# A new order of units, banks and cuts in the second attention of a fused two-block transformer kernel

## Chip, cores and metric

One core of a Trainium2 chip runs the whole program, one launch. The metric is the device time of one execution in microseconds. The kernel before takes 1139.63 us, the median of three runs (1139.48 to 1142.15).

## The reference

Two blocks of a transformer on 256 tokens of width 1024, float32 throughout. The first has three attentions (stick-breaking, forgetting, and one over a memory), gates and a relu-squared feed-forward. The second block has two layers. Its first layer is the one that matters here: an attention with 16 heads of 64 in 4 groups, with three branches whose outputs are gated and added.

```python
q = rms_norm(parts[0].reshape(B, T, G, HG, DH), q_norm)
kc, vc, ksl, vsl, kw, vw = [a.reshape(B, T, G, DH) for a in parts[1:7]]
...
k_cmp = rms_norm(compress(kc, pos_k, k_w1, k_b1, k_w2), kcmp_norm)   # gelu(blk @ w1 + b1) @ w2
v_cmp = compress(vc, pos_v, v_w1, v_b1, v_w2)
...
o = gb[..., 0:1] * o_c + gb[..., 1:2] * o_s + gb[..., 2:3] * o_w
...
x = x + o @ w_out
```

At 256 tokens the selected branch (o_s) and the window branch (o_w) both see every earlier position; the compressed branch (o_c) sees 15 compressed keys for each group. After it come a gated feed-forward, a second attention layer and a second feed-forward.

## The kernel before

The program is written by hand for each engine, as five instruction streams that meet at semaphores: `tensor_program`, `scalar_program`, `vector_program`, `gpsimd_program`, `sync_program`. Each stream is in order: an instruction that waits holds up all behind it on its engine. Nothing plans the order; it is the order of the text, and the loops over `i` in the four compute programs are meant to run side by side.

Weights stream through three raw buffers (`m.raw`), 1 MB a chunk, loaded by SyncE in the order of `CHUNKS`. Each chunk is cut into a rounded high part (ScalarE, `cut`) and a rest (VectorE, `cut`), and TensorE's `gemm` multiplies three pairs of high and low parts (lines 579, 581, 582). A raw buffer comes free when VectorE has cut its chunk. Chunks 84 to 87 hold the two compression weights and are used raw, by the products `hidden(n)` (line 906), 16 for the keys into bank 0 and 16 for the values into bank 1. Chunks 88 to 91 are the four blocks of the output projection `nwo`: 88 and 89 its first k half for output halves 0 and 1, 90 and 91 the second.

The attention is 32 units, in the order that `nsa_units` gives. A unit `main` computes the selected and the window branch for one head (token half 1, 256 keys) or two heads (token half 0, 128 keys); a unit `few` computes the compressed branch for four heads. Head block 0 comes first (units 0 to 11), then head block 1 (12 to 15 for token half 0, and from 16 on for token half 1), with the `few` units of block 0 placed between those of the last group.

The loop `for i in range(35)` runs in four streams:

- TensorE: in step i the scores of unit i into bank 6 or 7 (lines 663 and 674), then the transposes of the exponents of unit i-2 (line 559), then some filling work (`gemm` pieces or `hidden`), then the values of unit i-3 (line 694), then other transposes. A unit that opens an output group takes that group's bank, and waits until the group that held it has been read. In the steps of `late_opens` the values of unit i-4 and i-3 come together, a step late.
- VectorE: in step i a split or `stacked_...` where one is due, the maximum of unit i (line 1926), the copy of the transposed rows of unit i-2 out of PSUM (line 1938, every third is ScalarE's), the `join` of a group that ended with unit i-3 (reciprocal, gates, two passes that read the two output banks, one addition; in `late_joins` with unit i-4), then `hidden`, then a quarter of a `cut`.
- ScalarE: placing and splits, the exponents of unit i (line 1189), tanh, a quarter of a `cut` (line 1192).
- GpSimd: the gelu chains (`cubic`, `gelu`) and the scaling of the compressed keys.

Output groups lie in banks by `O_BANKS`: each entry is the bank of a group in the order in which the groups first appear. Transposes go through two spare banks, 4 and 5, in turn, among them `turn_out`, which transposes the joined output for the projection. Line 1769 is VectorE's helper for every tensor_tensor, 1192 ScalarE's copy, 2422 GpSimd's tensor_tensor.

Of the kernel before, what the change touches and what calls it, by code (L numbers as in the profile page):

```python
# [108 lines left out]
def bank_pairs():  # L109

    at, turn = {}, 0
    for name, kt, widths in GEMMS:
        if name in ("flog", "ngate", "cmpk", "cmpv"):
            continue
        for b in range(len(widths)):
# [7 lines left out]
            if name == "nwo":  # L123
                at[name, b] = ((3, 0), (1, 7))[b]
# [310 lines left out]
def nsa_units():  # L435
    main, few = {}, {}
# [8 lines left out]
    units = [*a, *b, *c, *d[:3], e[0], d[3], e[1], d[4], f[0], d[5], f[1], *d[6:], *g, *z]  # L445
# [19 lines left out]
O_BANKS = {"fox": (2, 3), "nsa": (2, 3, 2, 3, 2, 3, 0, 1, 2, 2, 2, 2), "mla": (2, 3)}  # L465
# [69 lines left out]
def tensor_program(e, m, book):  # L535
# [446 lines left out]
    late_opens = [u.i + 4 for u in NSA[4:] if u.kind == "main" and u.opens and u.i < 16]  # L982
    for i in range(35):
# [14 lines left out]
        elif 11 <= i < 17:  # L998
            for n in range(3 * i - 17 - max(0, i - 15), 3 * i - 14 - max(0, i - 14)):
                hidden(n)  # L1000
        elif 27 <= i < 31:
            gemm(88, lo_out, ready_out, (0,), (i - 27,))
# [17 lines left out]
        elif i in (12, 15):  # L1020
            turn_queries(1, 1, i // 15)
        elif i in (13, 19):
            turn_hidden(i // 19)
        elif i in (14, 20):
            compressed(i // 20)
        elif i == 17:
            w.wait_ge(*after("keys copied"))
            turn(("kst",), [m.kst[:]])
        elif i in (25, 29):
            turn_out(0, (i - 25) // 4)  # L1030
# [148 lines left out]
def scalar_program(e, m, book):  # L1179
# [379 lines left out]
    for i in range(35):  # L1559
# [6 lines left out]
        elif i in (13, 16):  # L1566
            place_queries(1, 1, i // 16)
        elif i in (14, 20):
            hidden(i // 20)
# [8 lines left out]
        elif i == 21:  # L1578
            w.wait_ge(*after("on", "cmp", 1))
            copy(m.vc[:], bank("cmp", 1)[0:60, 0:64]).then_inc(*out(("off", "cmp", 1)))  # L1580
        elif i in (26, 30):
            split(("no", 0, (i - 26) // 4), m.o_lo[0][:, :, half((i - 26) // 4)])
# [13 lines left out]
        elif i in (12, 18):  # L1596
            tanh(i // 18)
        if 11 <= i < 15:
            cut(88, i - 11)
        elif 20 <= i < 28:  # L1600
            cut(89 + (i - 20) // 4, (i - 20) % 4)
        elif 28 <= i < 32:
            cut(91, i - 28)
# [156 lines left out]
def vector_program(e, m, book):  # L1760
# [411 lines left out]
    for i in range(35):  # L2172
# [6 lines left out]
        elif i in (13, 16):  # L2179
            stacked_queries(1, 1, i // 16)  # L2180
        elif i in (26, 30):
            split(("no", 0, (i - 26) // 4), both(m.o_lo, 0, 4, (i - 26) // 4))
        elif i == 34:
            split(("no", 1, 0), both(m.HT, 4, 8, 0))
        if i < 32:
            maximum(NSA[i])
        if i == 18:
# [713 lines left out]
```

## Time and profile before

| | |
|---|---|
| median of three runs | 1139.63 us (1139.48 to 1142.15) |
| the profiled execution | 1142.15 us |
| its span, first to last instruction | 1140.3 us |
| TensorE matmuls busy | 1116.6 us, 98% |
| TensorE weight loads busy | 936.1 us, 82% |
| VectorE, ScalarE, GpSimd busy | 54%, 51%, 15% |
| granted TensorE clock | 0.999 |

Times in the timeline are microseconds from the span's start. A bracket at the end of a row is the time that the engine stood idle before it and the instruction that ended the wait. The ends of matmuls are modelled, and matmuls overlap, so the distance from one start to the next says more than a matmul's own duration. The loop of the second attention lies at about 548 to 650 us.

### The profile page before, as it was taken

The numbers are of one execution on the slowest core, as the hardware profiler recorded it, in microseconds if no ns is written. First come the engines' busy times: TensorE is split into PE (matmuls) and PEld (weight loads), VectorE is DVE, ScalarE is ACT, GpSimd is POOL, SyncE is SP. The second block draws the span as 40 slices with busy tenths as digits, with TensorE's granted clock in tenths as the row PEclk, the third lists the DMA queues.
The fourth block names the chain that finished last, engine by engine and source line by source line (L and its number), as shares of the span: only waits on it lengthen the run. The fifth ranks groups of instructions, "written<-read, shape, count | busy, mean of one in ns | idle before, by whom it ended". The sixth has DMA issues, their size and how long they took to land.

```text
span 1140.3 us, 14182 instructions
## 1 busy us (share of the span) xinstructions
PE 1116.6 (98%) x5899; PEld 936.1 (82%) x5899; DVE 620.1 (54%) x655; ACT 577.9 (51%) x891; POOL 171.0 (15%) x222
## 2 busy tenths in 40 slices
PE   6999999999999999999999999999999999999998
PEld 5777778888899988888878888888888687888887
DVE  5444454557645445457657665555456646555542
ACT  5688655443555534346567354444447635444431
POOL 1022111111131200032311000000017921000000
PEclk9999999999999999999999999999999999999999
DMA  9533333345554554545122255554544225555552
GB/s 340 203 116 143 147 116 144 132 166 192 202 200 166 212 184 185 189 155 185 59 98 88 75 184 184 185 184 166 184 151 162 76 111 191 187 184 191 183 170 77
DMA packets 28384, 184.34 MB, mean 162 GB/s; under 512 B 3472, under 2 KB 3856, under 8 KB 8080
## 3 DMA queue, kind: packets, MB, share of 16 engines
q1 hardware_dynamic: 26496, 177.52, 43.1%
q0 software_dynamic: 1824, 5.92, 1.5%
q8 instruction: 46, 0.75, 0.3%
q14 instruction: 18, 0.15, 0.0%
HBM read 182.38 MB, written 1.05 MB: 161 GB/s over the span
## 4 chain that ended last, share of the span: by engine, by line
PE 92%; ACT 3%; DVE 2%; POOL 2%; DMA 1%; issue 0%; POOLq 0%; DVEq 0%
PE ps L579 23%; PE ps L581 23%; PE ps L582 23%; PE ps L559 6%; PE ps L694 4%; PE ps L674 3%; PE ps L612 3%; PE ps L611 3%; PE ps L610 3%; POOL t L2422 2%; DVE t L1769 1%; ACT t L1192 1%; PE ps L906 1%; ACT t L1189 1%; DMA t<-in_g 1%; ACT L1189 1%
## 5 line engine op out<-in xcount | busy, mean ns | idle before, releaser
L1769 DVE TENSOR_TENSOR t<-t 128x2048 fp32r<-128x2048 f32 (+6 forms) x259 | 411.0, 1597 | 347.8 <-ACT t L1192 335.5
L579 PE MATMUL ps<-t 128*128 128x512 f32 (+2 forms) x1186 | 470.4, 397 | 4.0 <-DVE t L1769 2.7
L1192 ACT ACTIVATE t<-t 128x2048 fp32r<-128x2048 f32 (+5 forms) x220 | 323.5, 1485 | 278.3 <-PE ps L582 241.8
L581 PE MATMUL ps<-t 128*128 128x512 f32 (+2 forms) x1186 | 461.9, 389 | 0.6 <-POOL t L2422 0.6
L582 PE MATMUL ps<-t 128*128 128x512 f32 (+2 forms) x1186 | 462.1, 390 | 0.0
L579 PEld LDWEIGHTS ps<-t 128*128 128x128 f32 x1186 | 223.9, 189 | 48.5 <-DVE t L1769 5.1
L582 PEld LDWEIGHTS ps<-t 128*128 128x128 f32 x1186 | 223.7, 189 | 46.6
L581 PEld LDWEIGHTS ps<-t 128*128 128x128 f32 x1186 | 224.1, 189 | 44.3 <-POOL t L2422 1.1
L2422 POOL TENSOR_TENSOR t<-t 128x32 f32<-128x32 f32 (+10 forms) x127 | 122.2, 977 | 487.5 <-ACT t L1189 423.4
L1189 ACT ACTIVATE t<-ps,t 128x256 f32<-128x256 f32 (+4 forms) x216 | 95.9, 453 | 104.3 <-DVE t L1926 47.5
L559 PE MATMUL ps<-t 128*128 128x128 f32 (+3 forms) x667 | 96.4, 275 | 14.4 <-DVE t L1769 10.5
L1192 ACT ACTIVATE t<-ps 128x512 fp32r<-128x512 f32 (+8 forms) x106 | 57.3, 560 | 94.7 <-PE ps L559 89.0
L559 PEld LDWEIGHTS ps<-t 128*128 128x128 f32 (+3 forms) x667 | 77.9, 137 | 30.8 <-issue 14.1
L1769 DVE TENSOR_TENSOR t<-ps,t 128x512 fp32r<-128x512 f32 (+5 forms) x132 | 81.5, 638 | 35.1 <-ACT t L1192 31.9
L610 PE MATMUL ps<-t 128*128 128x256 f32 x256 | 72.5, 283 | 0.0
L612 PE MATMUL ps<-t 128*128 128x256 f32 x256 | 72.5, 283 | 0.0
L611 PE MATMUL ps<-t 128*128 128x256 f32 x256 | 72.4, 283 | 0.0
L1192 ACT ACTIVATE t<-ps,t 128x512 f32<-128x512 f32 (+5 forms) x75 | 44.9, 645 | 31.8 <-PE ps L559 22.4
L674 PE MATMUL ps<-t 128*128 128x256 f32 (+5 forms) x240 | 53.4, 343 | 0.3 <-DVE t L2322 0.3
L694 PEld LDWEIGHTS ps<-t 128*128 128x128 f32 (+1 forms) x384 | 46.8, 191 | 5.8 <-issue 4.5
L694 PE MATMUL ps<-t 128*128 128x64 f32 (+2 forms) x384 | 49.8, 274 | 0.0
L611 PEld LDWEIGHTS ps<-t 128*128 128x128 f32 x256 | 49.1, 192 | 0.0
(98 smaller groups left out, 536.3 us busy)
## 6 DMA issues: line engine op xcount, KB each, us to landing
t<-in_w SPq DMA_DIRECT2D x158, 1024.0 KB, 4.9
t<-in_w SPq DMA_DIRECT2D x8, 512.0 KB, 3.5
t<-in_w SPq DMA_DIRECT2D x5, 768.0 KB, 4.3
t<-in_g POOLq DMA_DIRECT2D x6, 512.0 KB, 5.7
t<-in_w SPq DMA_DIRECT2D x2, 640.0 KB, 3.8
t<-in_x SPq DMA_DIRECT2D x4, 256.0 KB, 5.9
t<-in_mem POOLq DMA_DIRECT2D x1, 1024.0 KB, 9.8
out<-t SPq DMA_DIRECT2D x4, 256.0 KB, 4.5
```

Source lines behind the costliest of these rows:

```text
L559: t = e.transpose(ps[0:n, j * 128:j * 128 + rows], s, m.ident[0:rows, 0:rows])
L579: e.matmul(o, sh, wh, start=k0 + j == 0, stop=False)
L581: e.matmul(o, sh, wl, start=False, stop=False)
L582: t = e.matmul(o, sl, wh, start=False, stop=last and j == n - 1)
L610: e.matmul(o, wh, hi, start=k == 0 and f == 0, stop=False, skip_group_check=True)
L611: e.matmul(o, wh, lo, start=False, stop=False, skip_group_check=True)
L612: t = e.matmul(o, wl, hi, start=False, stop=k == 7 and f == 1, skip_group_check=True)
L694: t = e.matmul(bank[k][:, o:o + v.shape[1]], PT[u.i % len(PT)][0:rows, z * 128:(z + 1) * 128], v, start=c == 0, stop=c == len(blocks) - 1)
L1189: return e.activation(o, src, f, **k)
L1192: return e.activation(o, src, ACT.Copy, scale=scale)
L1769: return e.tensor_tensor(o, a, b, op)
L2422: return e.tensor_tensor(o, a, b, op)
```

## The change

The order of the units: the first `few` unit moves from place 19 to 20, and the others of block 0 from 21, 23 and 25 to 22, 24 and 26. The banks: the groups of block 1, token half 1, go to banks 2 and 3 in place of 0 and 1, the compressed groups to bank 1 in place of 2, and the projection's outputs to 0, 2, 3, 7 in place of 3, 0, 1, 7. Unit 16's values become one of the late ones, in step 20. The `hidden` products of the values' compression are spread over steps 11 to 17, and what follows from them moves by a step. VectorE's stacked compressed keys come ahead of the maximum in step 18. The output transposes of block 0 and their splits move a step later. The cuts of chunks 88 to 90 now run without a pause, on ScalarE in steps 12 to 23 and on VectorE in 13 to 24, and those of chunk 91 a step earlier.

```diff
--- before.py
+++ after.py
@@ -121,7 +121,7 @@
             if name == "nsc":
                 at[name, b] = (2, 3)
             if name == "nwo":
-                at[name, b] = ((3, 0), (1, 7))[b]
+                at[name, b] = ((0, 2), (3, 7))[b]
             if name == "mwo":
                 at[name, b] = ((0, 1), (6, 7))[b]
             if name == "qa":
@@ -442,7 +442,7 @@
             few[hg, h] = [Unit("nsa", "few", 0, h, tuple(range(u0, u0 + 4)), 60, hg, 4) for u0 in (0, 4)]
     a, b, c, d = main[0, 0], main[0, 1], main[1, 0], main[1, 1]
     e, f, g, z = few[0, 0], few[0, 1], few[1, 0], few[1, 1]
-    units = [*a, *b, *c, *d[:3], e[0], d[3], e[1], d[4], f[0], d[5], f[1], *d[6:], *g, *z]
+    units = [*a, *b, *c, *d[:4], e[0], d[4], e[1], d[5], f[0], d[6], f[1], d[7], *g, *z]
     return numbered(units)
 
 
@@ -462,7 +462,7 @@
 LAST_OF_FIRST = max(u.i for u in NSA if u.block == 0)
 MLA, MLA_GROUPS = mla_units()
 S_BANKS = {"fox": lambda i: (6, 7)[i % 2], "nsa": lambda i: (6, 7)[i % 2], "mla": lambda i: (6, 7)[i % 2]}
-O_BANKS = {"fox": (2, 3), "nsa": (2, 3, 2, 3, 2, 3, 0, 1, 2, 2, 2, 2), "mla": (2, 3)}
+O_BANKS = {"fox": (2, 3), "nsa": (2, 3, 2, 3, 2, 3, 2, 3, 1, 1, 1, 1), "mla": (2, 3)}
 
 
 def queries_of(m, u, n):
@@ -979,7 +979,7 @@
     def ready_out(k, h):
         return after("off", "no", k // 4, h)
 
-    late_opens = [u.i + 4 for u in NSA[4:] if u.kind == "main" and u.opens and u.i < 16]
+    late_opens = [u.i + 4 for u in NSA[4:] if u.kind == "main" and u.opens]
     for i in range(35):
         if i < 32:
             nsa_scores(NSA[i])
@@ -995,11 +995,11 @@
         elif 7 <= i < 11:
             for n in range(4 * i - 28, 4 * i - 24):
                 hidden(n)
-        elif 11 <= i < 17:
-            for n in range(3 * i - 17 - max(0, i - 15), 3 * i - 14 - max(0, i - 14)):
+        elif 11 <= i < 18:
+            for n in range(2 * i - 6 + max(0, i - 16), min(2 * i - 4 + max(0, i - 15), 32)):
                 hidden(n)
-        elif 27 <= i < 31:
-            gemm(88, lo_out, ready_out, (0,), (i - 27,))
+        elif 28 <= i < 31:
+            gemm(88, lo_out, ready_out, (0,), ((0,), (1,), (2, 3))[i - 28])
         elif i == 31:
             gemm(89, lo_out, ready_out, (0,))
         elif i == 33:
@@ -1017,17 +1017,17 @@
             turn_queries(0, 1, i - 2)
         elif i in (9, 10):
             turn_queries(1, 0, i - 9)
-        elif i in (12, 15):
-            turn_queries(1, 1, i // 15)
-        elif i in (13, 19):
-            turn_hidden(i // 19)
-        elif i in (14, 20):
-            compressed(i // 20)
+        elif i in (12, 16):
+            turn_queries(1, 1, i // 16)
+        elif i in (13, 20):
+            turn_hidden(i // 20)
+        elif i in (14, 21):
+            compressed(i // 21)
         elif i == 17:
             w.wait_ge(*after("keys copied"))
             turn(("kst",), [m.kst[:]])
-        elif i in (25, 29):
-            turn_out(0, (i - 25) // 4)
+        elif i in (26, 30):
+            turn_out(0, (i - 26) // 4)
     gemm(90, lo_out, ready_out, (0,))
     turn_out(1, 1)
     gemm(91, lo_out, ready_out, (0,))
@@ -1563,10 +1563,10 @@
             place_queries(0, 1, i - 3)
         elif i in (10, 11):
             place_queries(1, 0, i - 10)
-        elif i in (13, 16):
-            place_queries(1, 1, i // 16)
-        elif i in (14, 20):
-            hidden(i // 20)
+        elif i in (13, 17):
+            place_queries(1, 1, i // 17)
+        elif i in (14, 21):
+            hidden(i // 21)
         elif i == 15:
             o = bank("cmp", 0)[0:60, 0:64]
             w.wait_ge(*after("on", "cmp", 0))
@@ -1575,11 +1575,11 @@
         elif i == 18:
             w.wait_ge(*after("on", "kst"))
             copy(m.cA[:], bank("kst")[:, 0:60], m.cst("gnc")).then_inc(*rounded(("stacked", "kst")))
-        elif i == 21:
+        elif i == 22:
             w.wait_ge(*after("on", "cmp", 1))
             copy(m.vc[:], bank("cmp", 1)[0:60, 0:64]).then_inc(*out(("off", "cmp", 1)))
-        elif i in (26, 30):
-            split(("no", 0, (i - 26) // 4), m.o_lo[0][:, :, half((i - 26) // 4)])
+        elif i in (27, 31):
+            split(("no", 0, (i - 27) // 4), m.o_lo[0][:, :, half((i - 27) // 4)])
         elif i == 34:
             split(("no", 1, 0), m.HT[0][:, 4:8, half(0)])
         if 2 <= i < 34 and i - 2 in TURNED_BY_ACT:
@@ -1593,14 +1593,12 @@
                 copy(m.KD[i - 1][0:64, :, half(h)], p[0:64]).then_inc(*out(("off", "dup", i - 1, h)))
         elif i in (3, 5):
             squares_by_head("nsq1", 0, i // 4, 512)
-        elif i in (12, 18):
-            tanh(i // 18)
-        if 11 <= i < 15:
-            cut(88, i - 11)
-        elif 20 <= i < 28:
-            cut(89 + (i - 20) // 4, (i - 20) % 4)
-        elif 28 <= i < 32:
-            cut(91, i - 28)
+        elif i in (12, 19):
+            tanh(i // 19)
+        if 12 <= i < 24:
+            cut(88 + (i - 12) // 4, (i - 12) % 4)
+        elif 27 <= i < 31:
+            cut(91, i - 27)
     split(("no", 1, 1), m.HT[0][:, 4:8, half(1)])
     cut_by_piece(92)
     split_half("f1", 0, 0)
@@ -2176,21 +2174,21 @@
             stacked_queries(0, 1, i - 3)
         elif i in (10, 11):
             stacked_queries(1, 0, i - 10)
-        elif i in (13, 16):
-            stacked_queries(1, 1, i // 16)
-        elif i in (26, 30):
-            split(("no", 0, (i - 26) // 4), both(m.o_lo, 0, 4, (i - 26) // 4))
-        elif i == 34:
-            split(("no", 1, 0), both(m.HT, 4, 8, 0))
-        if i < 32:
-            maximum(NSA[i])
-        if i == 18:
+        elif i in (13, 17):
+            stacked_queries(1, 1, i // 17)
+        elif i == 18:
             p, a = bank("kst")[:, 0:60], m.cA
             w.wait_ge(*after("stacked", "kst"))
             e.tensor_copy(m.cB[0:64], bm(a[low_k].bitcast(F32), 2)).then_inc(*out(("copied",)))
             w.wait_ge(*after("copied"))
             e.scalar_tensor_tensor(out=a[low_k], in0=p[low_k], scalar=m.cst("gnc")[low_k], in1=a[low_k].bitcast(F32),
                                    op0=ALU.mult, op1=ALU.subtract).then_inc(*rests(("off", "kst")))
+        elif i in (27, 31):
+            split(("no", 0, (i - 27) // 4), both(m.o_lo, 0, 4, (i - 27) // 4))
+        elif i == 34:
+            split(("no", 1, 0), both(m.HT, 4, 8, 0))
+        if i < 32:
+            maximum(NSA[i])
         if 2 <= i < 34 and i - 2 not in TURNED_BY_ACT:
             copy_rows(NSA[i - 2], m.PT1)
         for n in (i - 3, i - 4):
@@ -2219,14 +2217,12 @@
         elif i == 8:
             w.wait_ge(*after("blocks", 0))
             scale_queries(1, 1)
-        elif i in (11, 17):
-            hidden(i // 17)
-        if 12 <= i < 16:
-            cut(88, i - 12)
-        elif 21 <= i < 29:
-            cut(89 + (i - 21) // 4, (i - 21) % 4)
-        elif 29 <= i < 33:
-            cut(91, i - 29)
+        elif i in (11, 18):
+            hidden(i // 18)
+        if 13 <= i < 25:
+            cut(88 + (i - 13) // 4, (i - 13) % 4)
+        elif 28 <= i < 32:
+            cut(91, i - 28)
     add_and_gain_half("nwo", 0, 0, "f1", G_FF0, ("no", 0, 0))
     split(("no", 1, 1), both(m.HT, 4, 8, 1))
     cut_by_piece(92)
```

## Rows read from the trace of the kernel before

**Rows 1.** The page's first part: busy us, share of the span, count, by engine

```profile
PE 1116.6 (98%) x5899; PEld 936.1 (82%) x5899; DVE 620.1 (54%) x655; ACT 577.9 (51%) x891; POOL 171.0 (15%) x222
```

**Rows 2.** Busy time by stretch: us, then by engine, clock, DMA share, GB/s

```profile
548.00:620.00 72.00, 71.98 (x507) 58.54 (x506) 47.51 (x86) 46.16 (x170) 15.52 (x25) 1.00 0.25 87
620.00:650.00 30.00, 28.80 (x191) 24.21 (x190) 19.46 (x39) 11.94 (x50) 0.00 (x0) 1.00 0.25 93
```

**Rows 3.** Timeline of TensorE's matmuls, steps 27 and 31 (start, us, line, shape)

```profile
619.81 0.28 PE L663 MATMUL ps<-t 128*128 128x256 bf16 x1
...
620.98 0.63 PE L559 MATMUL ps<-t 128*60 128x128 f32 x4 [0.42 <-DVE t L1769]
...
632.69 0.27 PE L663 MATMUL ps<-t 128*128 128x240 bf16 x1
...
633.61 0.62 PE L559 MATMUL ps<-t 128*60 128x128 f32 x4
635.01 0.50 PE L579 MATMUL ps<-t 128*128 128x512 f32 x1 [0.78 <-DVE t L1769]
```

**Rows 4.** Timeline of TensorE's matmuls, steps 11 and 16 to 19

```profile
576.01 1.51 PE L906 MATMUL ps<-t 128*60 128x256 f32 x6
...
593.81 0.60 PE L559 MATMUL ps<-t 128*128 128x128 f32 x4
594.35 1.07 PE L906 MATMUL ps<-t 128*60 128x256 f32 x4
595.35 2.00 PE L694 MATMUL ps<-t 128*128 128x64 f32 x16
...
599.34 0.28 PE L663 MATMUL ps<-t 128*128 128x256 bf16 x1
...
599.93 0.60 PE L559 MATMUL ps<-t 128*128 128x128 f32 x4
600.37 1.00 PE L694 MATMUL ps<-t 128*128 128x64 f32 x8
601.21 0.27 PE L663 MATMUL ps<-t 128*128 128x240 bf16 x1
...
602.23 0.66 PE L559 MATMUL ps<-t 128*128 128x128 f32 x4
```

**Rows 5.** Timeline of VectorE, steps 15, 17, 18, 26 and 30

```profile
592.61 0.24 DVE L2158 RECIPROCAL t<-t 128x16 f32<-128x16 f32 x1
...
593.10 1.29 DVE L1769 TENSOR_TENSOR t<-ps,t 128x512 f32<-128x512 f32 x2
...
599.28 0.42 DVE L1769 TENSOR_TENSOR t<-ps,t 60x256 f32<-60x256 f32 x1
600.13 0.69 DVE L1926 TENSOR_REDUCE t<-ps 128x2 f32<-128x512 f32 x1 [0.43 <-PE ps L674]
600.74 0.22 DVE L2190 CAST t<-t 64x120 fp32r<-64x120 f32 x1
...
601.18 0.67 DVE L1938 COPY t<-ps 128x512 f32<-128x512 f32 x1
...
620.23 0.69 DVE L1769 TENSOR_TENSOR t<-ps,t 128x512 fp32r<-128x512 f32 x1 [1.75 <-ACT t L1192]
...
633.18 0.23 DVE L2158 RECIPROCAL t<-t 128x16 f32<-128x16 f32 x1
...
633.67 1.29 DVE L1769 TENSOR_TENSOR t<-ps,t 128x512 f32<-128x512 f32 x2
```

**Rows 6.** Timeline of ScalarE, step 18

```profile
599.60 0.31 ACT L1192 ACTIVATE t<-ps,t 128x60 fp32r<-128x60 f32 x1
```

**Rows 7.** Timeline of GpSimd, the last step of the second gelu

```profile
602.75 0.72 POOL L2422 TENSOR_TENSOR t<-t 60x256 f32<-60x256 f32 x1
```

**Rows 8.** DMA issues from 570 to 660 us: count, KB each, us to landing

```profile
t<-in_w SPq DMA_DIRECT2D x8, 1024.0 KB, 4.8
```

## The prediction

> **What bounds the kernel now.** The summary comes first [rows 1]: TensorE is counted busy for 98% of the span, VectorE and ScalarE for about half. So the change, which touches only the order of the second attention (the 35 steps of `for i in range(35)`), can gain only what TensorE waits there. The table of stretches [rows 2] covers these steps: TensorE's matmuls are busy for 71.98 of 72 us in the first stretch and 28.80 of 30 in the second, at a clock of 1.00. The missing 1.2 us are the two brackets in the timeline of matmuls [rows 3]: 0.42 in front of transposes, 0.78 in front of block 89, both released by a VectorE tensor_tensor.
>
> Since a modelled end can hide a wait, I price by the distance from one start to the next [rows 3]. The four transposes of step 27 start 1.17 us after the scores of the step began (619.81 to 620.98), where step 18 has 0.59 (599.34 to 599.93 [rows 4]): 0.58 us waited. The bank they want still holds the first output transposes, which VectorE's split leaves at 620.23 plus 0.69, and that split had itself waited 1.75 us for ScalarE's half [rows 5]. In step 31 block 89 starts 1.40 us after the transposes (633.61 to 635.01), where four transposes take 0.44 (599.93 to 600.37): 0.96 us. It takes a bank that VectorE's join of unit 27 frees at 633.67 plus 1.29 [rows 5]. Together some 1.6 us, the whole known stock of waits that this change could win.
>
> The Trainium skill (Perfetto Trace Analysis, Identifying the Most-Contended Engine) says that matmul busy time is a poor measure of how near TensorE is to its limit and that weight-load busy time is a better one. Here the weight loads are busy for 82.75 of 102 us [rows 2], so by that rule up to 19 us would be open rather than 1.6.
>
> **The change, part by part.** The matrix work is the same in kind and count: 32 units of scores, transposes and values, 32 `hidden` products, projection blocks 88 to 91. Only places move.
>
> (a) The second `hidden` run is spread over seven steps (11 to 17: 2,2,2,2,2,3,3) instead of six (3,3,3,3,2,2). Three products take 1.51 us and two take 1.07 [rows 4], so 0.44 for one; two with all that belongs to them last from 594.35 to 595.35, so 0.12 are a run's own. The transposes ahead of a run take 0.54 (593.81 to 594.35) instead of 0.44 (599.93 to 600.37). One run more costs 0.12 + 0.10, some **+0.2 us**. The lighter steps 11 to 15 start sooner by a product each, and so do the maxima and the late join of unit 11, which frees banks 2 and 3 at 593.10 plus 1.29 in before [rows 5], 0.96 us ahead of the values at 595.35. In after, the query transposes leave step 15 for step 16 behind the values, and the two hidden products of step 16 become three, so join and values both come earlier by about as much. Nothing there; if that margin were gone, the loss would stand in step 16, and its bounds are 0 and 0.5 (the transposes that left).
>
> (b) Block 1's second half now accumulates in banks 2 and 3, which its first half (unit 15 the last) still holds, and opens at step 20 (`late_opens` gains 20). Before, it opened banks 0 and 1 in step 19 and waited for nobody. VectorE still joins unit 15 in step 19. TensorE's side of the walk [rows 4]: step 19 started at 601.21, now at 601.4 by (a). Full scores take 0.59 (599.34 to 599.93), transposes 0.44, and no values follow: 602.4. Step 20: the small scores take 0.92 (632.69 to 633.61 [rows 3]), then transposes 0.44: at 603.8 it asks for banks 2 and 3.
> VectorE's side [rows 5]: the stacked keys of step 18 go first now. ScalarE's copy of them ends at 599.91 [rows 6], and both VectorE operations take 0.44 (600.74 to 601.18): about 600.4. Maximum 0.61 (600.13 to 600.74): 601.0. Copy of rows, 0.6 when the next stands behind it (its row says 0.67): 601.6. Then `hidden`, 0.42, moved here from step 17: 602.1. Then a quarter of the cut of block 89, moved here from step 22, a 512-column pass like the copy, 0.6: 602.7. Step 19: maximum 0.61, 603.3; the join frees both banks 1.78 us after its start (592.61 to 593.10 plus 1.29): 605.1. So TensorE waits 605.1 - 603.8, a new wait: **+1.3 us**. It is 0.6 if VectorE comes to the join with no backlog (602.0 + 0.61 + 1.78 = 604.4), and 2.5 if the cuts of steps 16 and 17 and the later query placing (two passes of 0.6) leave VectorE one pass or two further behind. What is queued behind the join on VectorE is the cut of step 19 and the maximum of unit 20; its exponents and transposes are due on TensorE only in step 22, two steps later, and a step is 1.9 (0.59 + 0.44 + 0.84, the last from 600.37 to 601.21) to 2.2 us, so no second wait follows. The gelu chain took in before 3.8 us, from the end of VectorE's `hidden` at 599.70 to GpSimd's last product at 602.75 plus 0.72 [rows 7]. From 602.1 that is 605.9. TensorE asks for it in step 20 behind the values of units 16 and 17, at 605.1 + 1.7 = 606.8, and finds it done; were the banks free it would ask at 605.5 and wait 0.4 instead.
>
> The Trainium skill (Perfetto Trace Analysis, Optimizing Tensor Performance, Matmuls) says that independent groups should rotate through different PSUM banks, so that emptying one overlaps the next. Part (b) ends one such rotation, and the walk gives it a price of the same sign; by the rule alone, without a duration, only the sign would be known.
>
> (c) The first small unit moves from 19 to 20, and the stacked keys come before the maximum. In before its scores took 1.02 us (601.21 to 602.23 [rows 4]) against the 0.92 of a later one, while VectorE did the keys: **-0.1 us**.
>
> (d) Output transposes move from steps 25 and 29 to 26 and 30, their splits to 27 and 31, and the cuts of blocks 89 to 91 to four or one step earlier. Between the first output transposes and the next user of their bank lies now one small scores (0.92) in place of a full one (0.59): 0.3 us more cover. VectorE waited for ScalarE's half, which in before had a cut ahead of it in step 25 and has none now. Of the 0.58 us I take **-0.5** (bounds 0 and -0.6). In step 30 VectorE no longer has the second split (0.69 as the first) ahead of the maximum and the join. The join of unit 27 can't start before its values end at 632.69 [rows 3], and it started at 633.18 [rows 5]: **-0.45** (bounds 0 and -0.5). The rest of that wait, 0.5, is the join itself, which block 89 still needs. Block 88's first half goes in three runs rather than four, in the same count of matmuls; a run's own cost in (a) bounds it at -0.1, and I take nothing.
>
> (e) SyncE: the raw buffers of blocks 92 to 94 come free with the cuts, one to four steps earlier, and block 90's with the last `hidden`, one step later. Transfers land 4.8 us after issue [rows 8] and block 90 is cut from step 20 on, three steps (some 6 us) after step 17. No wait of TensorE in these stretches is on a transfer. Nothing; were that cover gone, ScalarE would be 1 or 2 us late with block 90, which TensorE reads only after step 34.
>
> Sum: 0.2 + 1.3 - 0.1 - 0.5 - 0.45 = **+0.45 us**, on a profiled execution of 1142.15 us (span 1140.3, 1.85 around it). The median of the three runs is 1139.63, 2.5 lower than the profiled one, and the difference goes on the median: **1140.1 us**.
>
> **The rivals.** *The waits only move* (forecast): about 1 us either way of +0.45. Under 0.3% (3.4 us, about what a measurement of this kernel can tell from no change), so it counts as the same.
> *VectorE falls behind in steps 16 to 20* and TensorE waits in 20 and again after it. For it: the cuts now run without a pause from 13 to 24, and step 18 puts 0.44 + 0.61 + 0.6 + 0.42 + 0.6 = 2.7 us on VectorE against TensorE's 1.9. Against: from step 20 VectorE has 1.2 to 1.8 us a step (two or three passes of 0.6) against 1.9 to 2.2 for TensorE, so the lag is worked off. Price: 2.5 for the bank and no gain in the tail, +0.2: +2.7, 1142.3. It decides from 0.8 us more, that is if the gelu chain, which ScalarE's tanh shares with exponents that come late, ends past 607.6 rather than at 605.9: then 1143.1 and beyond, slower.
> *Faster*: the bank wait is covered and both tail waits vanish whole: 0.2 - 0.1 - 1.6 = -1.5, 1138.1, still the same by the bound. Only by hidden waits could it be faster by more than 3.4 us: a fifth of the 19 us in which weight loads stand still, giving 1136.2 or less. Against it: the same kinds of work take nearly the same distance in different steps [rows 3, 4] (0.92 and 1.02 for small scores, 0.44 to 0.54 for transposes) but for the two waits named, which hidden waits of differing length would not leave so.
> *Nothing of the order matters*, since the same products bind TensorE: 1139.6.
>
> **How the numbers follow.** Waits only move, or nothing matters: 0.86. VectorE behind, within the bound: 0.04, past it: 0.05. Faster beyond the bound: 0.03; -1.5 us: 0.02. So faster 0.03, same 0.92, slower 0.05. The bounds of the parts give -0.5 (0.2 + 0.6 - 0.1 - 0.6 - 0.5 - 0.1) to +3.1 (0.2 + 2.5 - 0.1 + 0.5). The three runs themselves spread from 1139.48 to 1142.15, and I let the low end reach the -1.5 case and stop the high end at the rival's +2.7. Range: 1138.0 to 1142.3.
>
> **What would show it.** In the new profile TensorE should show one wait of 0.6 to 2.5 us before the values of the 17th unit (a run of sixteen L694 matmuls, the first in banks 2 and 3), released by VectorE's tensor_tensor; the wait for the bank of the first output transposes gone or under 0.2, that before block 89 near 0.5. `hidden` products should stand in eleven runs. Wrong would be: no wait at step 20, a wait on ScalarE or GpSimd's gelu of over 1 us, or starts in steps 11 to 16 that widen.

## The result

The changed kernel takes 1156.78 us (median of 4; 1155.03 to 1159.22), the kernel before 1140.14 beside it (median of 4). The ratio is 1.0144, with a 95% interval of 1.0117 to 1.0172: slower by 16.6 us, where 0.5 was forecast.

### The profile page after: what moved, and what is told of

It reads as the page before. It is cut to its first block, busy times and chain, and to the rows that moved or that the text cites. A ratio compares the mean times of both kernels' runs of the same rounds, so it can differ in the third digit from the quotient of the medians.

```text
span 1153.4 us, 14184 instructions
## 1 busy us (share of the span) xinstructions
PE 1128.9 (98%) x5899; PEld 947.1 (82%) x5899; DVE 620.8 (54%) x655; ACT 578.4 (50%) x891; POOL 171.7 (15%) x222
## 4 chain that ended last, share of the span: by engine, by line
PE 92%; ACT 3%; DVE 2%; POOL 2%; DMA 1%; issue 0%; SPq 0%; POOLq 0%; ACTq 0%; DVEq 0%
PE ps L579 22%; PE ps L582 22%; PE ps L581 22%; PE ps L559 6%; PE ps L694 4%; PE ps L674 3%; PE ps L612 3%; PE ps L610 3%; PE ps L611 3%; POOL t L2418 2%; ACT t L1192 1%; PE ps L906 1%; DVE t L1767 1%; ACT t L1189 1%; DMA t<-in_w 1%; PE ps L663 1%
## 5 line engine op out<-in xcount | busy, mean ns | idle before, releaser
L1767 DVE TENSOR_TENSOR t<-t 128x2048 fp32r<-128x2048 f32 (+5 forms) x259 | 411.3, 1598 | 347.5 <-ACT t L1192 335.8
L579 PEld LDWEIGHTS ps<-t 128*128 128x128 f32 x1186 | 223.5, 188 | 48.0 <-DVE t L1767 4.9
L582 PEld LDWEIGHTS ps<-t 128*128 128x128 f32 x1186 | 223.2, 188 | 46.4
L581 PEld LDWEIGHTS ps<-t 128*128 128x128 f32 x1186 | 223.6, 189 | 44.1 <-POOL t L2418 1.1
L559 PE MATMUL ps<-t 128*128 128x128 f32 (+3 forms) x667 | 99.9, 282 | 13.3 <-DVE t L1767 9.4
L559 PEld LDWEIGHTS ps<-t 128*128 128x128 f32 (+3 forms) x667 | 80.5, 141 | 29.9 <-issue 14.1
L694 PEld LDWEIGHTS ps<-t 128*128 128x128 f32 (+1 forms) x384 | 52.9, 212 | 8.0 <-issue 4.7
L674 PE MATMUL ps<-t 128*128 128x256 f32 (+5 forms) x240 | 57.8, 364 | 0.3 <-DVE t L2318 0.3
L694 PE MATMUL ps<-t 128*128 128x64 f32 (+2 forms) x384 | 55.9, 296 | 1.3 <-DVE t L1767 1.3
L1924 DVE TENSOR_REDUCE t<-ps 128x2 f32<-128x512 f32 (+2 forms) x48 | 30.7, 640 | 36.2 <-PE ps L674 35.9
```

Of the source, the lines that this page charges most:

```text
L559: t = e.transpose(ps[0:n, j * 128:j * 128 + rows], s, m.ident[0:rows, 0:rows])
L579: e.matmul(o, sh, wh, start=k0 + j == 0, stop=False)
L581: e.matmul(o, sh, wl, start=False, stop=False)
L582: t = e.matmul(o, sl, wh, start=False, stop=last and j == n - 1)
L694: t = e.matmul(bank[k][:, o:o + v.shape[1]], PT[u.i % len(PT)][0:rows, z * 128:(z + 1) * 128], v, start=c == 0, stop=c == len(blocks) - 1)
L1767: return e.tensor_tensor(o, a, b, op)
```

## The profile after

The page of the changed kernel, its span, its busy time by engine and the granted clock in 40 slices:

```profile
span 1153.4 us, 14184 instructions
...
PE 1128.9 (98%) x5899; PEld 947.1 (82%) x5899; DVE 620.8 (54%) x655; ACT 578.4 (50%) x891; POOL 171.7 (15%) x222
...
PEclk9999999999999999999995999999999999999999
```

Beside [rows 1], TensorE has 12.3 us more busy time for the same 5899 matmuls, and VectorE and ScalarE have the same as before within 1 us. So TensorE did not wait 13 us longer: its work took longer. One slice of the granted clock, in tenths of full speed, says 5; a slice is 28.8 us (1153.4 over 40).

The table of stretches of the same kernel, cut where the clock changes (us, busy time of TensorE, weight loads, VectorE, ScalarE, GpSimd, then clock, DMA share and GB/s):

```profile
548.00:604.40 56.40, 54.27 (x360) 41.71 (x360) 36.32 (x68) 35.17 (x121) 13.01 (x24) 1.00 0.30 105
604.40:635.10 30.70, 30.70 (x139) 27.46 (x138) 14.31 (x25) 12.20 (x53) 0.91 (x1) 0.50 0.20 69
635.10:650.00 14.90, 14.84 (x109) 13.22 (x109) 9.92 (x21) 7.91 (x34) 0.00 (x0) 1.00 0.00 1
```

For 30.7 us TensorE has half its clock, 1.2 GHz in place of 2.4, and is busy the whole time. In [rows 2] the clock is 1.00 over the whole loop. Below, the work of this loop is called narrow: transposes of 128 columns, values of 64 and small scores of 60, with wider full scores (one matmul of 256 columns, two of 512) only in about every second step. Wide stands for matmuls of 512 columns back to back. What stands ahead of the fall is in the timeline of matmuls, steps 19, 20 and 27:

```profile
599.66 0.60 PE L559 MATMUL ps<-t 128*128 128x128 f32 x4
601.08 0.28 PE L663 MATMUL ps<-t 128*128 128x240 bf16 x1 [0.81 <-ACT t L1189]
...
602.01 0.66 PE L559 MATMUL ps<-t 128*128 128x128 f32 x4
603.95 3.17 PE L694 MATMUL ps<-t 128*128 128x64 f32 x16 [1.29 <-DVE t L1767]
607.05 0.47 PE L559 MATMUL ps<-t 60*128 60x60 f32 x2
...
632.24 1.06 PE L559 MATMUL ps<-t 128*128 128x128 f32 x4
633.09 0.42 PE L663 MATMUL ps<-t 128*128 128x256 bf16 x1
...
635.15 1.11 PE L694 MATMUL ps<-t 60*128 60x64 f32 x8
```

TensorE stands still twice in step 20. From the transposes of step 19 to the small scores it is 1.42 us, of which the transposes take 0.44: 0.98 us for the exponents of unit 18. From the transposes of step 20 to the sixteen value matmuls it is 1.94, of which transposes there take 0.49 (602.23 [rows 4] to 602.72, where that timeline has values next): 1.45 us for the join of unit 15. The sixteen matmuls themselves start at the full clock and end at the half one (3.17 us, 2.00 in [rows 4]). From then on eight value matmuls take 1.8 us instead of 1.0.

VectorE and ScalarE ahead of the two waits:

```profile
594.27 1.25 ACT L1192 ACTIVATE t<-ps,t 128x512 fp32r<-128x512 f32 x2
597.07 0.48 ACT L1189 ACTIVATE t<-ps,t 128x256 f32<-128x256 f32 x1 [1.55 <-DVE t L1924]
...
597.98 0.63 ACT L1192 ACTIVATE t<-t 128x512 fp32r<-128x512 f32 x1
598.50 0.31 ACT L1192 ACTIVATE t<-ps,t 128x60 fp32r<-128x60 f32 x1
600.00 0.47 ACT L1189 ACTIVATE t<-ps,t 128x256 f32<-128x256 f32 x1 [1.19 <-DVE t L1924]
```

```profile
595.55 0.76 DVE L2061 SCALAR_TENSOR_TENSOR t<-ps,t 64x512 fp32r<-64x512 f32 x1 [2.79 <-ACT t L1192]
596.34 0.69 DVE L1924 TENSOR_REDUCE t<-ps 128x2 f32<-128x512 f32 x1
...
597.66 0.69 DVE L1767 TENSOR_TENSOR t<-t 128x512 fp32r<-128x512 f32 x1
598.85 0.21 DVE L2182 CAST t<-t 64x120 fp32r<-64x120 f32 x1 [0.49 <-ACT t L1192]
...
599.29 0.68 DVE L1924 TENSOR_REDUCE t<-ps 128x2 f32<-128x512 f32 x1
...
602.02 0.23 DVE L2156 RECIPROCAL t<-t 128x16 f32<-128x16 f32 x1
...
602.52 1.29 DVE L1767 TENSOR_TENSOR t<-ps,t 128x512 f32<-128x512 f32 x2
```

The delay builds up in three stages. VectorE idles 2.79 us until ScalarE has placed the last queries (594.27 plus 1.25), whose transposes now stand behind the values of step 16. So the maximum of unit 17 (596.34) and the exponents behind it (597.07) are late. Then a quarter of a cut (597.98) stands ahead of ScalarE's copy of the stacked keys, which ends at 598.81 (598.50 plus 0.31). Only then does VectorE go on to the keys and, at 599.29, the maximum of unit 18. The exponents start at 600.00, and the join frees the banks at 603.81.

## The experiments

Theory A: the waits of step 20 lower TensorE's clock, and the narrow matmuls of this loop then run at half speed until something denser comes. Theory B: the new order itself, narrow work massed together, lowers it. Below, a standstill is a distance between two starts less the time that the same work takes without a wait.

**banks_back**, the change with the banks and the opening step undone:

```diff
-O_BANKS = {... "nsa": (2, 3, 2, 3, 2, 3, 2, 3, 1, 1, 1, 1) ...}
+O_BANKS = {... "nsa": (2, 3, 2, 3, 2, 3, 0, 1, 2, 2, 2, 2) ...}
-late_opens = [u.i + 4 for u in NSA[4:] if u.kind == "main" and u.opens]
+late_opens = [u.i + 4 for u in NSA[4:] if u.kind == "main" and u.opens and u.i < 16]
```

> The changed kernel with one part undone: the output groups of block 1, token half 1, lie in banks 0 and 1 again, the compressed groups in 2, the projection in 3, 0, 1, 7, and unit 16 opens in step 19 again. Everything else of the change stays. Theory A (the wait for banks 2 and 3 in step 20 lets TensorE's granted clock fall to 1.2 GHz, and the narrow matmuls of this loop then run at half speed for some 30 us): no wait of over 0.5 us at steps 19 and 20, the clock stays at 1.00 from 560 to 650, and the time is that of the kernel before or up to 1 us less, 1139 to 1140.5. Theory B (the new order itself, with narrow work massed in steps 19 to 26 and fewer wide products in steps 11 to 15, lowers the clock): it still falls, 1153 to 1158.

Measured: 1153.72 us, ratio 1.0117 (1.0098 to 1.0136). My expectation of theory A, that without the new banks there is no wait, was wrong. Its timeline of matmuls:

```profile
600.39 1.10 PE L694 MATMUL ps<-t 128*128 128x64 f32 x8 [0.67 <-DVE t L1767]
...
604.81 0.33 PE L559 MATMUL ps<-t 60*128 60x60 f32 x2 [1.06 <-POOL t L2418]
...
606.28 0.66 PE L559 MATMUL ps<-t 128*128 128x128 f32 x4 [0.46 <-DVE t L1936]
```

TensorE waits for bank 1, which VectorE's `hidden` leaves late, then for the gelu chain behind it, then for a spare bank. The clock falls 0.6 us after the last of the three and is low for 23.9 us. The banks decide only what TensorE waits for. This run doesn't part theory B from A.

**banks_only**, the same edit the other way round on the kernel before (new banks and step 20, nothing else).

> The kernel before with that one part of the change alone: the new banks and unit 16 in step 20; order of units, cuts and hidden products as before. Theory A: TensorE waits for the join of unit 15 in step 20, but VectorE comes to it with less behind it (no cut and no hidden product in steps 17 to 19), so the wait is 0.5 to 1.5 us instead of 1.5 plus 1.0; if that is enough for the clock to fall the time is 1150 to 1158, if not it is 1140 to 1141. Theory B: no fall, 1140 to 1141.

Measured: 1140.29 us (10 executions), ratio 1.0008 (0.9994 to 1.0021).

```profile
598.93 0.66 PE L559 MATMUL ps<-t 128*128 128x128 f32 x4
600.22 0.33 PE L559 MATMUL ps<-t 60*128 60x60 f32 x2 [0.63 <-POOL t L2422]
...
601.07 0.60 PE L559 MATMUL ps<-t 128*128 128x128 f32 x4
601.68 1.97 PE L694 MATMUL ps<-t 128*128 128x64 f32 x16
```

0.80 us are lost to the gelu chain (1.29 less 0.49) and 0.17 to the join (0.61 less 0.44). In the profiled execution the clock stays, as at the lower end of what theory A allowed. Three others had mean clocks of 0.997 (1145.41 us) and 0.998 (1143.32 and 1142.72), where no execution of before was under 0.999. So they had shorter falls somewhere; where, no profile shows.

**filler**, the whole change, with TensorE working where it waited:

```diff
+    def fill(n):
+        for _ in range(n):
+            e.matmul(bank[0], m.identb[:], m.maskb[:, 0:512], start=True, stop=True, skip_group_check=True)
     for i in range(35):
+        if i == 20:
+            fill(4)
...
+        if i == 20:
+            fill(6)
         if i in late_opens:
```

> The whole change, and in step 20 ten more matmuls of 512 bf16 columns into the free bank 0, four ahead of the small scores and six ahead of the values of unit 16, so that TensorE works in the place of its two waits; their results are used by nobody. Theory A: the clock stays at 1.00, and the time falls from 1156 to 1139 plus the waits and what the fillers add, 1140 to 1143. Theory B: the narrow stretch that follows is unchanged, so the clock falls all the same, 1155 to 1160.

Measured: 1141.29 us (10 executions, 1140.25 to 1143.08), ratio 1.0009 (1.0000 to 1.0019).

```profile
602.21 0.66 PE L559 MATMUL ps<-t 128*128 128x128 f32 x4
602.70 1.46 PE L984 MATMUL ps<-t 128*128 128x512 bf16 x6
604.14 1.97 PE L694 MATMUL ps<-t 128*128 128x64 f32 x16
```

The values of unit 16 start 1.93 us after the transposes, against 1.94 in the changed kernel, and VectorE's join frees the banks at 604.00, 0.14 us ahead of them, as in the changed kernel: the dependencies are as late as they were. But the sixteen matmuls take 1.97 us, and the clock stays at 1.00 for the whole loop. The same order of narrow work with the standstill filled costs at most 0.2%. So the order alone doesn't lower the clock, and theory B falls, with one reservation: the filling is itself wide work. A filling of narrow matmuls was not run, so whether any work in that place would do is not shown. That a standstill by itself is enough, without the new order, is what the next runs test.

**one_wait**, the kernel before with one wait of TensorE added:

```diff
+        if i == 19:
+            w.wait_ge(*after("off", "o", 1, 0, 2))
         if i in late_opens:
```

> The kernel before, with one wait added and nothing else: TensorE waits in step 19, ahead of the values of unit 16, until VectorE has read the outputs of unit 15 in its join, some 2.1 us after it would have gone on (602.7 to 604.8). Theory A: the clock falls within a few us of it and stays low for 25 to 40 us; 1150 to 1158. Theory B: the wait costs its own length, 1141 to 1142.5, clock 0.999.

Measured: 1154.94 us, ratio 1.0132 (1.0104 to 1.0160). The profile has the values of step 19 at 602.32 behind transposes at 599.66, 2.2 us of standstill, and the clock low for 27.3 us. One wait alone, and none of the change, costs 15.0 us, nearly what the change costs (16.6), and the two intervals overlap.

**pause_short** and **pause_long**, the kernel before with a pause in step 22, of two or seven tiny GpSimd operations:

```diff
+        if i == 22:
+            w.wait_ge(*after("paused"))
         if i in late_opens:
...
     gelu(1)
+    pause(("on", "P", "nsa", 20))
     rms("nwo")
```

> The kernel before, with one pause: in step 22 TensorE waits, after its transposes, for GpSimd to run two tiny operations (8 columns) that start when those transposes end. About 0.7 to 1.0 us of standstill in the narrow stretch, no part of the change. If the length of standstill in a narrow stretch decides (theory A): about that of banks_only (0.6 and 0.2 us, no fall), so the clock stays in most executions, 1140.5 to 1141.5, perhaps falls in some. If any standstill does it: 1150 to 1158.

> The same with seven operations in place of two: 2.0 to 2.7 us of standstill in step 22. Theory A: the clock falls soon behind it and comes back only about where the projection blocks run, some 20 to 30 us later; 1150 to 1157. Rival (what fell in step 20 had to do with the banks, the join or the exponents, not with the standstill): no fall, 1142 to 1143.

Measured: 1148.36 us (6 executions, 1144.52 to 1154.36), ratio 1.0071 (1.0044 to 1.0099), for the short one, and 1148.18 (4 executions), ratio 1.0072 (1.0049 to 1.0095), for the long one. The first fence is of pause_short, the second of pause_long:

```profile
607.12 0.60 PE L559 MATMUL ps<-t 128*128 128x128 f32 x4
608.72 1.10 PE L694 MATMUL ps<-t 60*128 60x64 f32 x8 [1.00 <-POOL t L2600]
```

```profile
609.74 1.10 PE L694 MATMUL ps<-t 60*128 60x64 f32 x8 [2.39 <-POOL t L2600]
...
623.11 1.06 PE L559 MATMUL ps<-t 128*128 128x128 f32 x4
623.97 0.42 PE L663 MATMUL ps<-t 128*128 128x256 bf16 x1
...
624.80 0.60 PE L559 MATMUL ps<-t 128*128 128x128 f32 x4
```

Both medians are 8 us above the kernel before, 1140.19 beside them. That is more than the standstills alone and less than the 10 us or more that the expectations had for a fall. The standstills are 1.1 us (1.60 less the 0.54 of such transposes [rows 4]) and 2.5 (2.99 less 0.54). The clock was low for 17.1 and 13.7 us. It fell at about 611 in both and came back at 628.4 and 624.5. So the equal times are made of different parts: of 8 us, the short pause is 1.1 and the slow work 7, the long pause 2.5 and the slow work 5.5. In these two profiles the longer standstill did not make the slow stretch longer, and in both the slow work costs more than the standstill. What comes on top of the standstill is the narrow work between the fall and the place of return. In pause_long that place, 624.5, lies behind the output transposes and full scores, as in the changed kernel (632.24 to 635.1); in pause_short it is one step later. Why there and not at earlier full scores, no run parts.

**pause_wide**, the long pause among matmuls of 512 columns, between chunks 104 and 105.

> The same seven operations, but the pause stands in the gated feed-forward behind this attention, between chunks 104 and 105, among matmuls of 512 columns. Theory A with its second half (what costs is not the fall but that the narrow work behind it does not bring the clock back): the clock falls in some or all executions, for 3 to 7 us, and the time is 1142 to 1147. If a fall always lasts 30 us: 1155 and more. If it depends on nothing but the pause's own length: 1142.

Measured: 1142.35 us (10 executions, 1140.96 to 1146.23), ratio 1.0019 (1.0007 to 1.0031), so 2.2 us, about the pause's own 1.8:

```profile
732.30 0.60 PE L559 MATMUL ps<-t 128*128 128x128 f32 x4
734.48 0.50 PE L579 MATMUL ps<-t 128*128 128x512 f32 x1 [1.58 <-POOL t L2600]
```

In the profiled execution the clock didn't fall there. Three others had mean clocks of 0.997 and 0.998, so short falls are likely in some. The time alone also fits a pause that costs only its own length.

The same profile has a fall of 3.4 us elsewhere, in the last attention of the program:

```profile
892.63 3.65 PE L674 MATMUL ps<-t 128*128 128x128 f32 x16 [0.32 <-DVE t L2324]
896.21 0.79 PE L579 MATMUL ps<-t 128*128 128x512 f32 x1
```

Ahead of it stand sixteen scores of 128 columns and a wait of only 0.32 us. The clock fell at 895.6 and came back at 899.0. The profiles of banks_back and cuts_back have the same at 907, behind the same scores. So not every fall has a standstill of about a microsecond ahead of it. What led to these three was not tested.

**cuts_back**, the change with blocks 89 to 91 cut in their old steps:

```diff
-        if 12 <= i < 24:
-            cut(88 + (i - 12) // 4, (i - 12) % 4)
+        if 12 <= i < 16:
+            cut(88, i - 12)
+        elif 20 <= i < 28:
+            cut(89 + (i - 20) // 4, (i - 20) % 4)
```

and in the same way on VectorE, a step later, and for block 91.

> The whole change, but the cuts of blocks 89 to 91 stand in the steps they had in the kernel before, so none on ScalarE from 16 to 19 nor on VectorE from 17 to 20. TensorE's two waits in step 20 (1.0 us for the exponents of unit 18, 1.5 us for the join) should shrink by some 0.5 and 0.9 us, to about 1.1 in all. Theory A: between banks_only (0.8 us in all, no fall) and the change (2.5, fall), so either mostly 1140 to 1141, or falls in part of the executions, spread from 1140 to 1155. If the cuts have no part in it: both waits and the fall stay, 1153 to 1157.

Measured: 1154.57 us (4 executions), ratio 1.0127 (1.0098 to 1.0156). The wait for the exponents is gone and the join's is 1.0 us (1.49 less 0.49). The clock falls all the same, for 27.3 us in the profile, and in all four executions. So the cuts made the wait for the exponents and part of the join's, but without them enough is left. The expectation had named either mostly no fall or one in part of the executions.

```profile
600.41 0.66 PE L559 MATMUL ps<-t 128*128 128x128 f32 x4
601.90 2.46 PE L694 MATMUL ps<-t 128*128 128x64 f32 x16 [0.84 <-DVE t L1769]
```

**cuts_only**, the kernel before with the new steps of the cuts alone.

> The kernel before with the new steps of the cuts alone (ScalarE 12 to 23 and 27 to 30, VectorE one later). Theory A: each quarter of a cut puts 0.5 to 0.6 us on ScalarE and VectorE in steps 17 to 20. The exponents of unit 18, the gelu chain and its transposes come later by up to 1.2 us, and the gelu transposes of step 19, which found their input only 0.2 us old, wait 0.5 to 1.5 us. A fall then, 1148 to 1157. If only the banks and the unit order make waits: 1139 to 1140.5.

Measured: 1139.70 us (10 executions), ratio 1.0000 (0.9990 to 1.0010). The fall that I expected isn't there: the gelu transposes wait 0.16 us and a later set 0.4. The cuts alone make no standstill that matters.

**mended**, cuts_back with the last query transposes in step 15 again:

```diff
-        elif i in (12, 16):
-            turn_queries(1, 1, i // 16)
+        elif i in (12, 15):
+            turn_queries(1, 1, i // 15)
```

> The change with the old steps for the cuts of blocks 89 to 91 and the last query transposes back in step 15, ahead of the values of units 12 and 13. In cuts_back the one wait left, 1.05 us for the join of unit 15, still brought the clock down; VectorE's stacked queries (0.6 us) and what waits for them come earlier now, so the wait should shrink to 0.3 to 0.6 us. Theory A: no fall, and of the change the shorter waits at the end of the loop remain: 1138.8 to 1140, at best 0.1% under the kernel before. If the wait stays near 1 us: 1150 to 1156.

Measured: six executions, 1141.61, 1142.35, 1155.86, 1155.92, 1159.14 and 1160.66 us. The profiled one is the first; its clock is 1.00 in this loop, with this wait:

```profile
602.83 0.65 PE L559 MATMUL ps<-t 128*128 128x128 f32 x4
604.20 1.97 PE L694 MATMUL ps<-t 128*128 128x64 f32 x16 [0.72 <-DVE t L1769]
```

0.9 us of standstill (1.37 less 0.49), where 0.3 to 0.6 was expected. The same program falls in four executions and doesn't in two. The four are known by their times and by granted clocks of 0.984 to 0.979 over the span, against 0.999. None of the four was profiled, so it isn't shown that their standstill was 0.9 us too.

**rewarm**, the whole change with its waits, and `fill(12)` in step 21, when the clock is low.

> The whole change with its waits and its fall, and twelve matmuls of 512 bf16 columns into the free bank 0 in step 21, when the clock is low; their results are used by nobody, they cost 5.1 us at 1.2 GHz. Theory A, second half (narrow work does not bring the clock back, wide back-to-back work does): the clock is back by about 614 instead of 635, which gives back some 10 us and costs 3 to 5: 1148 to 1152. If a fall has a fixed length of 14 to 30 us: 1159 to 1163.

Measured: 1149.57 us (4 executions), ratio 1.0078 (1.0061 to 1.0095), 7 us under the change.

```profile
604.35 3.48 PE L694 MATMUL ps<-t 128*128 128x64 f32 x16 [1.29 <-DVE t L1774]
...
610.05 3.41 PE L984 MATMUL ps<-t 128*128 128x512 bf16 x12
613.30 1.00 PE L694 MATMUL ps<-t 128*128 128x64 f32 x8
```

In this execution, the fastest of the four (1147.19 us), the clock was low for 6.8 us instead of 30.7. It came back at 611.4, within the wide matmuls, and the narrow ones behind them run at full speed. A fall has no fixed length. The other three had mean clocks of 0.993 and 0.994, against 0.997 here, so theirs was low for longer; how it went there, no profile shows.

**mended_fill**, mended with `fill(4)` ahead of the values of unit 16.

> mended, whose executions fell into two groups (1141.6 and 1142.4 without a fall in this loop, 1155.9 to 1160.7 with one), and four matmuls of 512 bf16 columns into the free bank 0 ahead of the values of unit 16, which take up the 0.9 us that TensorE stood still there; their results are used by nobody. Theory A: no execution falls, all in 1138.5 to 1143, ratio to the kernel before 0.999 to 1.001, since of the change only some 0.5 us of shorter waits at the loop's end are left. If something else than the standstill parts mended's executions: two groups again.

Measured: 1140.02 us (12 executions, 1138.62 to 1142.64), ratio 1.0006 (0.9998 to 1.0015). No execution of the upper group is left. So the fall of mended's four executions hung on the place where TensorE stood still, with the same reservation on wide work as for filler. It is also the best version of the new order, and it doesn't beat the kernel before.

| kernel | standstill near step 20 or 22, us | executions with the long fall |
|---|---|---|
| cuts_only | 0.2 and 0.4 | 0 of 10 |
| banks_only | 0.8 and 0.2 | 0 of 10 |
| mended | 0.9 (in one that didn't fall) | 4 of 6 |
| cuts_back | 1.0 | 4 of 4 |
| pause_short | 1.1 | 6 of 6 |
| one_wait | 2.2 | 4 of 4 |
| the change | 1.0 and 1.4 | 5 of 5, the profiled one among them |
| banks_back | 0.8, 1.1 and 0.6 | 4 of 4 |
| pause_long | 2.5 | 4 of 4 |
| filler, mended_fill | filled | 0 of 22 |

A fall counts as long where the mean clock of the span is 0.996 or less. That bound is drawn by hand and lies close between two executions: pause_short's of 1144.52 us, at 0.996, counts as fallen, and banks_only's of 1145.41, at 0.997, doesn't. The standstills go by one profile of each kernel, and they stand at different places with different work behind them. So the table gives a trend, more standstill and more falls, and no exact edge. Shorter falls could hide in the times of the rows with none.

## Why the prediction was wrong

**What failed first** is the assumption behind the sum, that a wait costs its own length. The text read "at a clock of 1.00" out of [rows 2] and then had no term for the clock. The missing term can be measured on the same work in two kernels, from the values of unit 16 to the small values of step 27. In the change that is 31.20 us (603.95 to 635.15), in mended_fill, at the full clock, 17.36:

```profile
602.43 1.97 PE L694 MATMUL ps<-t 128*128 128x64 f32 x16
...
619.79 1.10 PE L694 MATMUL ps<-t 60*128 60x64 f32 x8
```

So the fall costs 13.8 us, and some 2.4 are the two standstills themselves. Together 16.2, of the measured 16.6; the smaller terms are within the spread of the executions.

The trace of before had shown this price, 400 us ahead of the loop that I read. Its timeline and its table of stretches there:

```profile
154.88 0.76 PE L559 MATMUL ps<-t 128*128 128x128 f32 x4 [1.25 <-ACT t L1189]
155.29 0.78 PE L579 MATMUL ps<-t 128*128 128x512 f32 x1
```

```profile
155.50:158.50 3.00, 3.00 (x9) 2.35 (x9) 1.13 (x2) 2.53 (x6) 0.00 (x0) 0.50 0.00 0
159.00:160.00 1.00, 1.00 (x6) 0.80 (x5) 1.00 (x1) 0.00 (x0) 0.00 (x0) 1.00 0.06 16
```

A standstill in the first attention was followed at once by 3.4 us at half clock, which ended within 512-column matmuls. A mean clock of 0.999 over the span hides that. The 68 executions of before that ran beside the experiments fall into two groups: 47 of them took 1138.54 to 1140.75 us, 41 of these at a mean clock of 1.000, and 21 took 1141.20 to 1143.00, all at 0.999. So about a third probably had a short fall somewhere. Where, their times don't say: the profile of mended, also at 0.999, has it at 154.5 us, that of pause_wide at 895.6. The profiled execution of before (1142.15) is of the upper group, and the prediction took its 2.5 us over the median as spread.

With these rows the wait of 1.3 us that part (b) forecast would have had a second price: perhaps a fall, with the work behind it at half speed for at least the 3.4 us seen there, and in a stretch of other work for a time that no row bounded short of the loop's end. That is the rival that was missing.

The Trainium skill (TensorE: Matmul & The Clock Gate, HAM oscillation) describes the mechanism: a wait between groups of matmuls takes TensorE down to half its clock, the next group starts at the low clock, and that loss comes on top of the wait. The traces here agree in kind: the standstills are 2.4 us, and the slow stretch behind them costs 13.8 more. In the page's example the waits are on transfers and last some 3 to 5 us; here standstills of 0.98 and 1.45 us stood ahead of the fall.

**(a)** was right in kind. From the scores of step 11 to those of step 19 it is 26.6 us (572.50 to 599.09) against 26.3 before (574.90 to 601.21), so +0.3 where +0.2 was forecast. TensorE has no new wait there, and the late join of unit 11 kept its margin.

**(b)** had the place and the cause of the join's wait right, 1.45 us where 1.3 was forecast. It missed the other, 0.98 us for the exponents of unit 18. The failing line of the walk is "ScalarE's copy of them ends at 599.91", which was taken over from the trace of before. The walk put that copy 1.5 us ahead of the start of step 19 (599.91 against 601.4). In the change it ends only 0.3 us ahead of it (598.81 against 599.09), so 1.2 us late. Two things that the change moved stand in front of it: the placing of the last queries, which holds up the maximum and the exponents of unit 17, and a quarter of a cut. The prediction had both only in the upper bound of (b), as passes of VectorE and not as its wait for ScalarE. Everything that the walk set behind it on VectorE was late with it, the maximum of unit 18 first. The upper bound of (b), 2.5 us, is what the two waits came to together; that is luck, since it was a bound for the join's wait alone.

"so no second wait follows" was right by the trace, for a reason not foreseen: at half clock TensorE was the late one.

**(c)** was right: the small scores in step 20 take 0.93 us (601.08 to 602.01), where before they took 1.02. **(d)**: block 89 starts 0.69 us after its transposes in the change (647.36 to 648.05), where 0.38 is work (four transposes of this form, 128*60, in before from 620.98 to 621.36; the prediction's 0.44 is for 128*128): 0.3 us left, and 1.0 before by the same 0.38, so better than the 0.5 forecast. In mended_fill the wait of 0.58 us ahead of the transposes has become about 0.25 (618.35 to 619.20 less 0.59), so -0.3 where -0.5 was forecast. **(e)** no wait on a transfer, as forecast.

**The rivals.** "VectorE falls behind" named the place and the sign. Its price, at most 3.4 us and only by a chain of later waits, was wrong by the clock. "Faster" and "nothing of the order matters" fell with the measured time. At the full clock (mended_fill, filler) the new order is no faster than the old one either, so the 19 us of standing weight loads gave nothing.

## What to carry to other kernels

A wait of TensorE can have two prices, its own length and what the clock does behind it. So look at the granted clock in stretches of a few us over the whole trace of before, and note what stood ahead of each fall and what ended it. A stretch of narrow matmuls without wide ones near by is where a new wait of about a microsecond is dear; there, keep the margins of everything that a change delays, on every engine, and count what a moved instruction puts in front of rows that you take over from before. If a wait can't be avoided there, a few wide matmuls into a free bank in its place cost at most 0.2% here, and none of 22 executions had the long fall (filler, mended_fill).

## What was not expected of the hardware

- With matmuls busy for 30.70 of 30.70 us by the profile, and weight loads for 27.46, the clock stayed at 1.2 GHz. In rewarm it came back within twelve matmuls of 512 bf16 columns (3.41 us).
- 1.1 and 2.5 us of standstill at the same place cost the same 8 us, with 17.1 and 13.7 us at half clock behind them.
- The clock fell in four executions of six of one program (mended, 0.9 us of standstill in its profile), so a kernel near this edge has two times, here 1142 and 1156 to 1161 us.
- The clock also fell for 3.4 us behind sixteen scores of 128 columns with a wait of 0.3 us (last attention of the program, three of the profiles). The standstill of 1.25 us in the first attention lowered the clock in the profile of before and not in that of the change (1.00 from 153 to 160 us).
- What in the chip decides between two such executions stays open.
